# Output projection among the down products, and xT loads spread over gate-up pairs

## What is computed

```python
proj = x @ w_in                              # 1024 -> 1536
xp, zg = proj[..., :512], gelu(proj[..., 512:])
pool_out = (trailing means over 2/4/8/16 of xp, minus xp) @ pool_w * pool_scale
u, v = zg split in two;  v = LN(v)           # 512 wide
sgu_out = u * (lower_tri(w_s) @ v + b_s)     # within chunks of 128 positions
mix = concat(pool_out, sgu_out) @ w_out      # 1024 -> 1024
h = LN(alpha * x + mix)
y = LN(alpha * h + (silu(h @ w_gate) * (h @ w_up)) @ w_down)   # 1024 -> 2816 -> 1024
```

## Time and profile before

| | |
|---|---|
| Median of 3 runs | 2417.69 us (2414.22 to 2422.96) |
| The profiled execution's own time | 2416.68 us |
| Its span, from the first to the last instruction of the slowest core (core 5) | 2415.1 us |
| Busy on core 5: TensorE matmul, VectorE, ScalarE, GpSimd | 95%, 68%, 40%, 16% |
| HBM read and written, over the span | 246 GB/s |
| Mean granted TensorE clock, both dies | 0.983 |

### The profile page before, as it was taken

How to read it: one execution, slowest core, us unless ns; L and a number is a source line. 1 busy time by engine, 2 the same in 40 slices (tenths; PEclk the granted TensorE clock), 3 DMA queues, 4 the chain that set the end, 5 groups by cost and what they waited for, 6 DMA issues and landing times.

```text
span 2415.1 us, 48523 instructions; the slowest of 8 cores (2371.9 to 2415.1 us)
## 1 busy us (share of the span) xinstructions
PE 2285.5 (95%) x15738; PEld 1507.9 (62%) x15738; DVE 1632.7 (68%) x2681; ACT 977.9 (40%) x1747; POOL 391.7 (16%) x757
## 2 busy tenths in 40 slices
PE   6899999999999999999999999999999989999997
PEld 2344444665757667585765847667585765847684
DVE  1842345666777778767686776778767686776875
ACT  3331223534435353443534345353443534345351
POOL 3211123012020111102112020121102112020111
PEclk9999999999999999999999999999999999999999
DMA  9669977767796877868787786867868777686785
GB/s 169 188 142 184 199 189 209 258 202 226 256 280 238 252 233 239 272 213 243 242 226 248 238 255 233 240 223 255 274 220 241 242 222 252 227 254 235 249 297 194
DMA packets 189222, 558.86 MB, mean 231 GB/s; under 512 B 19760, under 2 KB 52016, under 8 KB 188976
## 3 DMA queue, kind: packets, MB, share of 16 engines
q1 hardware_dynamic: 172416, 517.45, 65.6%
q0 software_dynamic: 16560, 38.31, 11.0%
HBM read 529.50 MB, written 64.49 MB: 246 GB/s over the span
## 4 chain that ended last, share of the span: by engine, by line
PE 73%; DMA 15%; issue 4%; DVE 4%; ACT 2%; POOL 1%; DVEq 0%; SPq 0%; POOLq 0%; ACTq 0%
PE ps L914 34%; PE ps L1044 14%; DMA sb_wr<-scr_q 6%; PE ps L721 5%; DMA scr_gu<-sb_vn 4%; PE ps L990 4%; PE ps L550 4%; PE ps L571 4%; PE ps L528 4%; DMA sb_wr<-scr_gu 3%; PE ps L641 2%; PE ps L874 1%; ACT sb_junk L468 1%; DMA sb_wr<-xT 1%; PE ps L670 1%
## 5 line engine op out<-in xcount | busy, mean ns | idle before, releaser
L914 PE MATMUL ps<-sb_aS,sb_wr 128*128 128x256 f16 x4928 | 597.9, 273 | 17.8 <-ACT sb_tm L923 5.3
L914 PEld LDWEIGHTS ps<-sb_aS,sb_wr 128*128 128x128 f16 x4928 | 478.4, 98 | 100.1 <-issue 29.4
L914 PE MATMUL ps<-sb_hT,sb_wr 128*128 128x256 f16 x3696 | 454.8, 273 | 10.0 <-DMA sb_wr<-scr_gu 8.3
L914 PEld LDWEIGHTS ps<-sb_hT,sb_wr 128*128 128x128 f16 x3696 | 359.6, 98 | 70.9 <-issue 16.7
L923 ACT ACTIVATE sb_tm<-ps 128x512 f32<-128x512 f32 x462 | 270.9, 592 | 326.0 <-PE ps L914 310.5
L928 DVE TENSOR_TENSOR sb_tm<-sb_tm,ps 128x512 f32<-128x512 f32 x462 | 312.5, 681 | 79.2 <-PE ps L914 62.3
L933 ACT ACTIVATE sb_tm<-sb_tm 128x512 f32<-128x512 f32 x308 | 193.3, 628 | 279.5 <-DVE sb_tm L928 277.1
L1044 PE MATMUL ps<-sb_wr,sb_aS 128*128 128x512 f16 x1144 | 269.0, 385 | 4.3 <-DVE sb_aS L1027 1.9
L1044 PE MATMUL ps<-sb_wr,sb_aT 128*128 128x512 f16 x858 | 219.1, 399 | 44.9 <-DMA sb_wr<-scr_q 42.6
L970 DVE SCALAR_TENSOR_TENSOR sb_hr<-sb_hr,ps 128x512 f32<-128x512 f32 x206 | 132.3, 683 | 177.2 <-PE ps L1044 132.1
L468 ACT ACTIVATE sb_junk<-sb_hr,sb_nmu 128x1024 fp8e5<-128x1024 f32 x128 | 146.7, 1146 | 239.6 <-POOL sb_nmu L464 141.5
(11 more groups left out here) (122 smaller groups left out, 2768.9 us busy)
## 6 DMA issues: line engine op xcount, KB each, us to landing
sb_wr<-scr_gu SPq DMA_DIRECT2D x462, 512.0 KB, 5.4
sb_wr<-scr_s SPq DMA_DIRECT2D x104, 512.0 KB, 5.1
sb_wr<-scr_q SPq DMA_DIRECT2D x98, 512.0 KB, 5.1
sb_hr<-x SPq DMA_DIRECT2D x64, 512.0 KB, 7.4
out<-sb_hr SPq DMA_DIRECT2D x64, 512.0 KB, 7.6
sb_wr<-scr_o SPq DMA_DIRECT2D x44, 512.0 KB, 5.2
sb_wr<-scr_s SPq DMA_DIRECT2D x52, 384.0 KB, 5.0
sb_xT<-xT POOLq DMA_DIRECT2D x60, 256.0 KB, 10.4
```

The lines of the kernel that those rows point to most:

```text
L914: i = e.matmul(ps[:, bk.home, jj * 256:(jj + 1) * 256], lhsT=wr[:, s, c:c + 128], rhs=rhs[:, k, :], start=(k == 0 and new and jj == 0), st ...
```

## The change

Five things change, from macro tile 2 on.

- `out_proj` of mt + 1 no longer stands among gate-up pairs 8 and 9. Its two halves are called before the second and the fourth down product (`OUT_AT`), with places 23 and 26 instead of 16.1 and 18.1; the spatial gate S moves from 13.3 to 17.3, `norm1` from 22.5 to 28.5.
- The four sums of `mixT` no longer use `xT`: two lie in the buffer of v (`vn`), one in a row of `tm`, one in place in `mixT`.
- `load_xT` of mt + 2 moves from the down products to pairs 5 to 8 (`XT_AT`), one load a pair. Each load reads the name `go{mt}_{p}`, which the third product of pair p writes.
- The row sums for `norm1` are no longer made with the last adds of `out_proj`. All adds have one form (128x512), and a Copy with accumulation on ACT sums each block of `hr` at the head of `norm1`.
- `mixer` is called before pair 4, with SiLU after the last GELU as a hint; the sums of a have their place 3 before their product instead of 1.5.

```diff
--- before.py
+++ after.py
@@ -30,8 +30,9 @@
-OUT_AT = (8, 9)
+OUT_AT = (1, 3)
 OUT_FROM = 5
+XT_AT = (5, 6, 7, 8)
...
@@ -458,12 +459,12 @@
-        def ln_stats(r, b, src, n, reads, banks, pos, junk_, jname, after=()):
+        def ln_stats(r, b, src, n, reads, banks, pos, junk_, jname, after=(), one=False):
...
@@ -561,6 +563,7 @@
                 for t in silus[6:]:
                     t.after.append(last_gelu)
+                gelus[:] = [last_gelu]
...
@@ -658,7 +661,11 @@
-                ln_stats(r1, b, lambda hs=hs: hr[:, hs, :], D, [f"h{hs}"], [], q, junk[:], "junk", sums_of_a)
+                if mt >= OUT_FROM:
+                    P.add("act", lambda e, hs=hs, b=b: e.activation(
+                        out=junk[:], in_=hr[:, hs, :], func=AF.Copy, accum_out=sums_[:, r1, b, 0:1], saturate=False),
+                        c_act(1024) + 160, q, reads=[f"h{hs}"], writes=["junk", f"sm{r1}{b}0"], after=sums_of_a)
+                ln_stats(r1, b, lambda hs=hs: hr[:, hs, :], D, [f"h{hs}"], [], q, junk[:], "junk", sums_of_a, mt >= OUT_FROM)
...
@@ -679,19 +686,28 @@
-            oS = [xT[:, 2 * c:2 * c + 2, :].rearrange("p k (h t) -> p (k h) t", h=2) for c in range(4)]
...
-                for i, x0, x1, op in ((0, A[1][0], A[1][1], ALU.add), (1, oS[0], A[0][0], ALU.subtract),
-                                      (2, A[0][1], oS[1], ALU.subtract), (3, A[0][0], A[1][0], ALU.subtract)):
...
+                row = o_row[mt] = Bank("tm")
+                o_sum[:] = [(lambda i=i: vn[:].rearrange("p (i k h) t -> p i (k h t)", i=2, k=1)[:, i].rearrange(
+                    "p (k t) -> p k t", k=4)) for i in range(2)]
+                o_sum.append(lambda: tm[:, row.home, 0:512].bitcast(F16).rearrange("p (k t) -> p k t", k=4))
+                o_sum.append(lambda: A[1][0])
...
@@ -716,37 +732,25 @@
-                if not last:
-                    P.add("dve", lambda e, hs=hs, o=o, bk=bk, first=first: e.scalar_tensor_tensor(
...
-                    continue
-                for t in range(2):
-                    P.add("dve", lambda e, hs=hs + t, o=o, bk=bk, t=t, first=first, b=2 * i + t, m=2 * c + n:
...
-                              accum_out=sums_[:, r1, b, m:m + 1]), c_dve(256) + 100, q,
...
-            for b in range(4 * c):
-                P.add("pool", lambda e, b=b: e.tensor_tensor(out=sums_[:, r1, b, 0:2], in0=sums_[:, r1, b, 0:2],
...
+                P.add("dve", lambda e, hs=hs, o=o, bk=bk, first=first: e.scalar_tensor_tensor(
+                    out=hr[:, hs:hs + 2, o:o + 256], in0=hr[:, hs:hs + 2, o:o + 256],
...
@@ -932,7 +936,7 @@
-                    c_act(512), q + dq, banks=[t], tab="s"))
+                    c_act(512), q + dq, banks=[t], tab="s", after=gelus))
...
@@ -943,6 +947,7 @@
             before[:] = [prod("S1", "T1", Y, True, 0.4)]
+            before[0].writes.append(f"go{mt}_{p}")
...
@@ -994,12 +999,12 @@
-                    if mt > 0 and n == 1 and kg > 1 and mt + 2 < NMT:
+                    if mt == 1 and n == 1 and kg > 1 and mt + 2 < NMT:
                         load_xT(mt + 2, q, ks=[2 * (kg - 2)], after=last_dn)
...
@@ -1020,12 +1025,16 @@
             for pi, (c, lt, src, ch_, quarter) in enumerate(prods):
                 q0 = base + NJ + 1.7 * pi
+                if OUT_FROM <= mt + 1 < NMT and pi in OUT_AT:
+                    p = OUT_AT.index(pi)
+                    fetch_o(p, pos("O", p) - 5)
+                    out_proj(mt + 1, p, pos)
...
-                        out=aS[:, a2], in0=x0, in1=x1, op=op), c_dve(KH * 256, 2), q0 - 1.5,
+                        out=aS[:, a2], in0=x0, in1=x1, op=op), c_dve(KH * 256, 2), q0 - 3,
...
@@ -1049,8 +1058,6 @@
-                if 1 <= pi < 5 and mt + 2 < NMT:
-                    load_xT(mt + 2, q0, ks=[2 * pi - 2], after=last_dn)
...
@@ -1070,7 +1077,7 @@
-        offs_s = dict(offs, S=(13.3, 13.4, 13.5, 13.6), O=(16.1, 18.1), N=(22.5, 24.5, 26.5, 28.5))
+        offs_s = dict(offs, S=(17.3, 17.4, 17.5, 17.6), O=(23, 26), N=(28.5, 28.6, 28.7, 28.8))
...
@@ -1103,30 +1110,28 @@
             for p in range(NP):
-                if OUT_FROM <= mt + 1 < NMT and p in OUT_AT:
-                    c = OUT_AT.index(p)
-                    fetch_o(c, base + 2 * p - 8)
-                    if c == 0:
-                        mixer(mt + 1, pos)
-                    out_proj(mt + 1, c, pos)
+                if p == 4 and mt + 1 < NMT:
+                    mixer(mt + 1, pos)
                 up_pair(mt, p, base + 2 * p, before)
+                if p in XT_AT and mt + 2 < NMT:
+                    load_xT(mt + 2, base + 2 * p, reads=[f"go{mt}_{p}"], ks=[2 * XT_AT.index(p)])
...
```

More of the change, by code:

```diff
@@ L344, in build_nc @@
         junk = sb("junk", [128, D], mybir.dt.float8e5)
-        sums_ = sb("sums", [128, 4, 4, 4], F32)
+        sums_ = sb("sums", [128, 4, 4, 2], F32)
         nmu = sb("nmu", [128, 4, 4], F32)
@@ L459, in ln_slot @@
             return (ln_rr[0] - 1) % 4
-        def ln_stats(r, b, src, n, reads, banks, pos, junk_, jname, after=()):
+        def ln_stats(r, b, src, n, reads, banks, pos, junk_, jname, after=(), one=False):
             s0 = sums_[:, r, b, 0:1]
             P.add("pool", lambda e: e.tensor_scalar(
-                out=nmu[:, r, b:b + 1], in0=s0, scalar1=sums_[:, r, b, 1:2] if n == D else 0.0, scalar2=-1.0 / n,
-                op0=ALU.add, op1=ALU.mult), 300, pos, reads=[f"sm{r}{b}0", f"sm{r}{b}1"][:n // 512],
+                out=nmu[:, r, b:b + 1], in0=s0, scalar1=sums_[:, r, b, 1:2] if n == D and not one else 0.0, scalar2=-1.0 / n,
+                op0=ALU.add, op1=ALU.mult), 300, pos, reads=[f"sm{r}{b}0", f"sm{r}{b}1"][:1 if one else n // 512],
                 writes=[f"mu{r}{b}"], after=after)
@@ L686, in out_proj @@
                 ln1[mt] = ln_slot()
-                for i, x0, x1, op in ((0, A[1][0], A[1][1], ALU.add), (1, oS[0], A[0][0], ALU.subtract),
-                                      (2, A[0][1], oS[1], ALU.subtract), (3, A[0][0], A[1][0], ALU.subtract)):
[L689 to L692, removed]
+                row = o_row[mt] = Bank("tm")
[3 more added lines that the diff above has]
+                o_sum.append(lambda: A[1][0])
+                for i, x0, x1, op in ((0, lambda: A[1][0], lambda: A[1][1], ALU.add),
+                                      (1, o_sum[0], lambda: A[0][0], ALU.subtract),
+                                      (2, lambda: A[0][1], o_sum[1], ALU.subtract),
+                                      (3, lambda: A[0][0], lambda: A[1][0], ALU.subtract)):
+                    t_ = P.add("dve", lambda e, o=o_sum[i], x0=x0, x1=x1, op=op: e.tensor_tensor(
+                        out=o(), in0=x0(), in1=x1(), op=op), c_dve(1024, 2), q0 - 0.05,
+                        reads=mix + [[], ["vn0", "vn1"], ["vn2", "vn3"], []][i],
+                        writes=[["vn0", "vn1"], ["vn2", "vn3"], [], mix[0:4]][i],
+                        banks=[row] if i == 2 else (), alloc=[row] if i == 2 else ())
                 last_o[:] = [t_] + x7[-1:]
-            r1 = ln1[mt]
+            row = o_row[mt]
             def B(f, n):
@@ L724, in pe @@
                     return m
-                t_ = P.add("pe", pe, 8 * 108, q, reads=lt[1] + rt[1], banks=[bk], alloc=[bk] if new else (),
+                t_ = P.add("pe", pe, 8 * 108, q, reads=lt[1] + rt[1], banks=[bk] + [row] * (pi == 4), alloc=[bk] if new else (),
                            after=[xload[mt * 4 + b] for b in range(4)] + last_o)
                 last_o[:] = [t_]
-                first, last = left[quarter] == total[quarter], left[quarter] == 1
+                first = left[quarter] == total[quarter]
                 left[quarter] -= 1
@@ L1000, in down_plain, with down @@
                     z_add(mt, r, b, n, acc[b], True, True, q0 + n * NG + NG - 1)
-        def down(mt, base):
+        def down(mt, base, pos):
             r = ln2[mt] = ln_slot()
@@ L1105, in build_nc @@
             before = []
-            for lst in (silus, x1, x7):
+            for lst in (silus, x1, x7, gelus):
                 lst.clear()
@@ L1123, in build_nc @@
                 sums_of_a.clear()
-                for f in (mixer, out_plain, norm1):
+                for f in (out_plain, norm1):
                     f(mt + 1, pos)
@@ L1128, in build_nc @@
             else:
-                down(mt, base)
+                down(mt, base, pos)
             if OUT_FROM <= mt + 1 < NMT:
```

19 lines of the change are left out of this document (7 added, 12 removed).

## The result

The changed kernel takes 2383.32 us (median of 4 runs, 2375.99 to 2407.94) where the kernel before, run beside it, took 2417.35; the ratio is 0.9847, with an interval of 0.9813 to 0.9880. The forecast was 2374 us with a range of 2346 to 2406. Runs in which one die had a lower granted clock are left out of the ratio, and experiments whose whole time suffered from that are read by stages, on cores with a granted clock of 0.98 or more.

The account below looks back on a forecast made before the run. TensorE, busy 95% of core 5's span, was taken as the bound, with its waits winnable. Core 2: 2410.4 - 46 + 3 + 8 - 3 = 2372, given as 2374 us after span and median corrections; range 2346 to 2406.

Parts of the forecast that it names:

- The stall: Down products: without xT loads there a stage is 6.9 us shorter; 65 us on core 5, 46 on core 2.
- xT among the pairs: Gate-up pairs 5 to 8: xT loads beside the weights cost 0.3 us a stage, +3 us over eleven stages.
- Projection among down products: Down products: the output projection there gives down weights more time, 257 instead of 287 GB/s; gain priced at nothing.
- Tail of LayerNorm 1: End of the down stage: LayerNorm 1 starts later, exposing 0.7 us a stage, +8 us; bounds 0 and 8.4.
- Stages 2 and 3: Early stages mt = 2 and 3: getting xT earlier too saves 3 us, between 0 and 5.
- second rival: Gate-up: xT loads delay weights TensorE is about to use, so the collision moves along; 2410 to 2425 us, chance 0.05.
- The sum: Whole kernel: core 5 at 2358 us, core 2 slowest at 2372, given as 2374 us.
- (1): Start of each up stage: LayerNorm 1's tail replaces the stall; 2489 us, chance 0.07; milder form 2392 to 2410, chance 0.10.
- (2): Gate-up pairs: the collision of xT loads with weights moves there; 2410 to 2425 us, chance 0.05.
- (3): Seams between stages and core 2's early part: more than the stall is won, below 2350 us; chance 0.08.

Follow-up runs that it names:

- e7: Kernel before without the xT loads in its down products; no scr_q wait on core 0, 17.6 us before; times not read, granted clock lowered.
- e2: Changed kernel with the output projection back before gate-up pairs 8 and 9; a stage of 138.6 to 139.1 us on cores 4 to 7.
- e4: Changed kernel with the projection back in gate-up and row sums back on DVE; a stage of 138.3 to 138.8 us on cores 4 to 7.
- e1: Changed kernel with xT loads put back among the down products, without a semaphore; 2370.39 us profiled, stages of 139.1 to 139.9 us.
- e12: Changed kernel with all four xT loads issued together after the first down product, by semaphore; 2385.34 us, mean stage 140.6 to 141.0 us.
- e10: Changed kernel with the xT loads of stages 2 and 3 back in their down products; mt = 2 to 4 8.7 us shorter on average.
- e11: Kernel before with mix sums in v's buffer and xT loads of stages 4 to 13 in pairs 5 to 8; 2362.75 us, ratio 0.9772.

## Why the prediction was right, and where a term was wrong

**The stall.** Right. The forecast was a stage of 139 to 140 us (145.5 - 6.9 + 0.3 + 0.7 = 139.6); 139.1 was measured. Reading mt = 14, the stage without the suspect, as an experiment of the kernel itself gave the size to half a microsecond. That the loads were the cause is shown by mt = 14 and e7, where only they are gone, and borne out by e2 and e4, where they move and the projection doesn't. What was imprecise is how they came together and what parts them: I took the semaphores for the cure, and in e1 the loads spread without them, once POOL's order and the place of the sums were others. And a bunch doesn't stall in every setting (e12).

**xT among the pairs.** Priced at 0.3 us a stage. Right for mt = 4 on: core 5 has no scr_gu wait in 820 to 2275 us; cores 1, 3, 4 and 6 have 2.8 to 3.8 us in ten stages. That the lead of over 10 us hides the slower landing fits this.

**Projection among down products, priced at nothing.** Right with the loads moved (e2, e4: taking it back gains 0.5 to 0.7 us a stage), incomplete as a statement on the move: by itself it is a remedy (e12).

**Tail of LayerNorm 1.** Priced at 0.7 us a stage; the wait is 1.2. The mechanism is as forecast: the chain of sum, square, cast and copy on ACT ends just behind TensorE's own work, and a pooling product fills the gap. TensorE's timeline on core 3:

```profile
1131.32 1.89 PE L574 MATMUL ps<-sb_xT,sb_wp 128*128 128x512 f16 x8
...
1134.85 0.61 PE L677 MATMUL ps<-sb_ident,sb_vn 128*128 128x128 f16 x8 [1.20 <-ACT sb_vn L670]
```

**Stages 2 and 3: the step that failed.** "Stages 2 and 3 get their xT earlier too; there I take 3 us off" has the wrong sign. The three stages mt = 2 to 4 together lost 7.1 us, where -3 for these two and about -2 for mt = 4 (3 off for its stall, 1 on for its tail and its xT) were forecast: an error of some 12 us. I had priced xT loads in gate-up from a later stage, and had not looked at the two that also sum the down weights; there TensorE waits 9.3 us for scr_gu on core 5, where it waited 4.3 before, and 3.4 us of that stand between 472 and 479 us, among the four xT loads issued from 461 to 478 us. It is the second rival's mechanism, in two stages instead of eleven; e10, without the xT loads there, wins 8.7 us back.

**The sum.** Core 5: forecast 2358, measured 2358.6, by errors that cancel: 57.5 us won in mt = 5 to 13 where 53 were forecast, and 3.6 us up to the end of mt = 1 where none was, but mt = 2 to 4 4.3 us longer. (mt = 14 is 2.8 us shorter and mt = 15 2.7 us longer.) Core 2: forecast 2372, measured 2363.4. Its stages fell by 143.16 - 139.19 = 4.0 us as its smaller stall lets expect; but it had ended mt = 1 only at 416.64 us before, against 402.44 on core 5, and that delay, which I carried over, was gone (401.29). It belonged to the execution and not to the kernel, as the windows of core 2 show, before and then after:

```profile
100.00:150.00 50.00, 47.88 (x230) 21.97 (x229) 35.76 (x58) 27.56 (x36) 19.38 (x24) 0.81 0.37 106
...
100.00:150.00 50.00, 45.25 (x247) 21.83 (x248) 32.74 (x51) 24.52 (x32) 16.56 (x20) 0.97 0.40 93
```

The granted clock was 0.81 there, where core 5 of the same execution had 0.97. The slowest core became core 3, whose mt = 2 to 4 take 457.5 us, the most of all. So that the profiled execution met 2374 so closely (2375.99), with the failed step in it, is luck. It is the lowest of the four runs; the median of 2383 lies 9 us over the forecast, well within its range.

**The rivals.** (1) The tail as a new bound: the wait is there, but 1.2 us and with a granted clock of 1.00; it needed 4.4. (2) The collision moved along only into stages 2 and 3. (3) Below 2350: no; beyond the stall only core 2's late start was won, and that was its granted clock.

## What to carry to other kernels

A stage that lacks the suspect is an experiment already in the trace: compare it first. Then price each edit in every kind of stage that it reaches, from the waits of that stage, and not only in the one that repeats. And before adding waits to spread transfers, look at what holds them together: here it was POOL's own order, behind the statistics of LayerNorm 1, while the buffer also served as scratch. Undo, too, the parts of a change one at a time: the smaller one (scratch elsewhere, loads moved only from mt = 4 on, the projection left where it was) beat the full one by some 0.8%.

## What the runs showed that was not expected

- A landing time of 8.0 us, which came with a stall of 4 us before, comes with none from mt = 5 on in e12: the landing alone says nothing. That the lead decides is argued.
- Taking the projection out of the down products (e4, e11) shortens mt = 7 and 11 to 135 to 137 us, while the other stages stay at 138 to 142; with the bunch (e12) the same two are the long ones, 143 to 146. The tile after them is the first of a sequence, with another mix; why it turns both ways wasn't tried.
- Before, the waits for scr_q from 820 to 2275 us are 17.6 to 30.2 us on cores 0 to 3 and 40.1 to 42.7 on cores 4 to 7, and the stages 142.3 to 143.2 and 144.8 to 145.5 us; after, they are 5.0 to 10.1 us, and 139.1 to 139.9 on all cores. So the stall is longer on cores 4 to 7; no run shows why.
